# A layer of a hybrid diffusion step on one core: the order in which expert weights are loaded, and four smaller reorderings

## The chip, the cores and the metric

The kernel runs on one NeuronCore of a Trainium2 chip (trn2). The metric is the device time of one execution in microseconds (us). All arithmetic is in 32-bit floats.

## The reference

One layer is computed for 128 context tokens and 512 latent tokens, each of 1024 features. It is an attention sublayer and then a mixture of 16 experts, with a modulation (six vectors of 1024 from a conditioning vector and `w_ada`) around both. Cut to what matters here:

```
def expert_choice_moe(h, w_router, w_gate, w_up, w_down):
    cap = CAPACITY_FACTOR * T // N_EXPERTS          # 64 latent, 16 context tokens for each expert
    logits = jnp.einsum('btd,de->bte', h, w_router, preferred_element_type=jnp.float32)
    aff = jax.nn.softmax(logits, axis=-1)
    g, idx = lax.top_k(jnp.swapaxes(aff, 1, 2), cap)
    xg = jax.vmap(lambda hb, ib: hb[ib])(h, idx)
    a = jnp.einsum('becd,edf->becf', xg, w_gate)
    u = jnp.einsum('becd,edf->becf', xg, w_up)
    y = jnp.einsum('becf,efd->becd', jax.nn.silu(a) * u, w_down) * g[..., None].astype(h.dtype)
    return (each token's rows of y, added up)

def ffn_sublayer(...):
    h = modulate(x, g_pre_ffn, shift, scale)
    return x + gate * rms_norm(expert_choice_moe(h, ...), g_post_ffn)
```

The attention has 16 query heads of 64: eight of group A (all keys, normed and rotated queries) and eight of group B (a window of neighbours and a learned sink). Gate, up and down are 1024x1024 for each expert, 4.2 MB each and 201 MB in all.

## The kernel before, in words

The program writes out by hand what each engine does in order; semaphores tie the engines together. PE is TensorE, ACT ScalarE, DVE VectorE, POOL GpSimd and SP the queue that issues most transfers. Tokens are in five tiles of 128: tile 0 is context, 1 to 4 are latent.

*Projection.* Fifteen passes (three windows of `w_in` by five tiles) make keys, values and queries. PE projects (line 655), turns the result in four blocks (`turn_qk`, L673), ACT copies the high part (`high_part`, L1155) and DVE subtracts it for the low part (`low_part`, L1497). Pass 14 is rotated late, by `rotate_last`.

*Attention.* 80 head units, 40 of group A (`u` from 0) and 40 of group B (from `A_UNITS` = 40; tile 0 comes first). A unit is: scores on PE (L704), `maxima` on DVE (L1569, L1576), exponentials on ACT (L1175), the division on DVE (L1675, L1676), `turn_probs` on PE (L738), `copy_pT` on ACT (L1269) and, each two units, `values` on PE (L760). Between the units of group B, PE does the output projection of the tile before (L809), the turning of the new rows (L822) and the router's logits, `route_logits` (L838). The router's weights times the modulation, `wrm`, are made by DVE at unit 2 (L1684).

*Gap.* The rest of the last tile's projection, then the choice of tokens: DVE finds each expert's 64 and 16 best (L1710 to L1713), POOL gathers their rows, PE turns them (`turn_rows_c`, `turn_rows_l`, L933). `keep_busy` is products whose results nobody reads. The context products of expert 0 come first, from weights loaded since attention's end.

*Experts.* Ring slots 0 to 5 hold two halves of 2 MB each of gate, up and down; slots 6 and 7 hold the gate of each second expert, so a gate is double buffered and up and down are not. PE goes up(e), gate(e+1), down(e), and each half is a context product (L966) and a latent product (L954) in four strips of 32 columns. SP refills a slot when PE has used it, in the order of its own program, and blocks at each wait:

```
def refill(e, kind, odd=False):
    used = ((gate_a, gate_b), (up_a, up_b), (down_a, down_b))[kind]
    for half in (0, 1):
        sp.wait_ge(used[half], e - 1 if kind == 0 else e)
        expert_weight(e, kind, half, SLOTS + half if odd else 2 * kind + half)
```

DVE weighs the result, POOL adds it to the sums in memory by an indirect transfer with addition.

*Tail.* SP reads the sums of the first 15 experts, DVE gates them (L1859), ACT squares them (L1354), POOL takes the root (L2032, L1923), DVE adds the tile (`add_x1`, L1864) and SP stores it. The last expert's rows go another way: `add_last` (L1871), `gain_last` (L1876), a product over the parts on PE (L1091), `mean_last` (L1880), a root, `rows_last_c` (L1887) and `rows_last_l` (L1893), and two indirect writes by POOL (L2039, L2043), which end the kernel.

## Time and profile before

| | us |
|---|---|
| three runs | 947.54, 947.57, 952.59 |
| median | 947.57 |
| the profiled execution | 948.19 |
| its span, first to last instruction | 946.2 |

Busy in the span: PE 884.3 us, the weight load beside it 442.2, DVE 365.8, ACT 216.5, POOL 102.6. The granted TensorE clock is 0.986 of full over the span. Busy time of PE is modelled: a product is shown from its start for a fixed time, so small waits hide in it, and the weight load's own waits (PEld) show them better. A slice of the page is 23.65 us.

### The profile page before, as it was taken

To read this page: it belongs to the slowest core of one execution; us is meant where nothing else is said; L and a number is where in the kernel's file an instruction comes from. 1 tells how busy PE (TensorE), PEld (TensorE's weight loads), DVE (VectorE), ACT (ScalarE), POOL (GpSimd) and SP (SyncE) were. 2 spreads that over 40 slices of the span, in tenths; PEclk is the share of its full clock that TensorE was granted. 3 is DMA by queue.
4 is the path that set the end of the run, shared out by engine and by line. 5 is a ranking of instruction groups with operands and counts; after the bars stand their busy time and mean duration, and the time that the engine had idled before them with its cause. 6 is when DMAs were issued, how large, how long until landed. Compare 5 with 4: busy or idle time off the path is not lost. (4 is left out here: it accounts for less than half of the span.)

```text
span 946.2 us, 19909 instructions
## 1 busy us (share of the span) xinstructions
PE 884.3 (93%) x8641; PEld 442.2 (47%) x8641; DVE 365.8 (39%) x977; ACT 216.5 (23%) x528; POOL 102.6 (11%) x137
## 2 busy tenths in 40 slices
PE   3999998899899999779999999999999999999984
PEld 3544444777656665533444443443444443433431
DVE  4255635888766766811112021121113120210126
ACT  3132223666645653400000000000000000000012
POOL 2021200000000000100110111011101101110225
PEclk9999999999999999899999999999999999999998
DMA  9997532300001116969999999999999999999983
GB/s 337 351 367 279 212 144 96 122 2 1 2 1 46 45 46 239 414 242 405 398 396 411 397 398 403 404 397 397 411 397 397 396 410 398 398 407 391 359 321 151
DMA packets 77717, 269.31 MB, mean 285 GB/s; under 512 B 6208, under 2 KB 9984, under 8 KB 77632
## 3 DMA queue, kind: packets, MB, share of 16 engines
q1 hardware_dynamic: 72384, 251.42, 67.8%
q0 software_dynamic: 4160, 13.90, 5.1%
q10 hardware_dynamic: 1088, 2.74, 0.7%
q8 instruction: 68, 1.11, 0.5%
q14 instruction: 17, 0.14, 0.0%
HBM read 252.06 MB, written 15.99 MB: 283 GB/s over the span
## 5 line engine op out<-in xcount | busy, mean ns | idle before, releaser
L954 PE MATMUL ps<-ring,reg 128*32 128x512 f32 x1792 | 201.6, 592 | 0.0
L1812 DVE TENSOR_SCALAR mod<-ps,kt 64x512 f32<-64x512 f32 x30 | 22.5, 750 | 255.9 <-PE ps L954 255.7
L954 PEld LDWEIGHTS ps<-ring,reg 128*32 128x32 f32 x1792 | 59.1, 110 | 111.8 <-issue 103.3
L966 PE MATMUL ps<-ring,values_in 128*32 128x256 f32 x1536 | 93.6, 386 | 4.0 <-issue 2.9
L1325 ACT ACTIVATE reg<-ps 128x256 f32<-128x256 f32 x16 | 6.1, 384 | 366.6 <-PE ps L1006 354.1
L954 PE MATMUL ps<-ring,kt 128*32 128x512 f32 x768 | 86.8, 592 | 0.0
L809 PE MATMUL ps<-ring,reg 128*128 128x512 f32 x160 | 76.4, 604 | 0.0
L966 PEld LDWEIGHTS ps<-ring,values_in 128*32 128x32 f32 x1536 | 50.0, 112 | 54.1 <-issue 24.8
L655 PE MATMUL ps<-ring,reg_qt 128*128 128x512 f32 x160 | 70.6, 594 | 0.0
L966 PE MATMUL ps<-ring,reg 128*32 128x256 f32 x1024 | 60.9, 379 | 2.5 <-DMA ring<-in_w_down 1.9
L1269 ACT ACTIVATE ring<-ps 128x640 f32<-128x640 f32 (+3 forms) x80 | 44.4, 555 | 72.5 <-PE ps L738 69.9
L738 PE MATMUL ps<-ident,ring 128*128 128x128 f32 x288 | 47.7, 285 | 14.0 <-DVE ring L1676 7.7
L1971 POOL TENSOR_TENSOR small<-mhalf 128x1 f32<-128x1 f32 x31 | 9.5, 306 | 460.1 <-DVE kt L1815 426.7
L1175 ACT ACTIVATE ring<-ps,small 128x640 f32<-128x640 f32 (+3 forms) x80 | 51.0, 638 | 7.9 <-DVE small L1576 7.9
L738 PEld LDWEIGHTS ps<-ident,ring 128*128 128x128 f32 x288 | 33.8, 144 | 37.2 <-issue 19.0
L966 PEld LDWEIGHTS ps<-ring,reg 128*32 128x32 f32 x1024 | 33.0, 110 | 36.8 <-issue 12.9
L954 PEld LDWEIGHTS ps<-ring,kt 128*32 128x32 f32 x768 | 25.4, 110 | 46.8 <-issue 42.8
L655 PEld LDWEIGHTS ps<-ring,reg_qt 128*128 128x128 f32 x160 | 29.6, 190 | 34.7 <-issue 34.7
L760 PE MATMUL ps<-ring,values_in 128*64 128x128 f32 x576 | 40.3, 280 | 0.6 <-ACT ring L1269 0.6
L809 PEld LDWEIGHTS ps<-ring,reg 128*128 128x128 f32 x160 | 28.5, 189 | 24.7 <-issue 24.0
L1676 DVE TENSOR_SCALAR ring<-ring,small 128x640 f32<-128x640 f32 (+3 forms) x80 | 36.8, 460 | 2.8
L631 PE MATMUL ps<-ring,reg_qt 128*128 128x512 f32 x80 | 35.9, 596 | 1.3 <-ACT reg_qt L1122 1.3
(235 smaller groups left out, 1000.7 us busy)
## 6 DMA issues: line engine op xcount, KB each, us to landing
ring<-in_w_up SPq DMA_DIRECT2D x32, 2048.0 KB, 22.7
ring<-in_w_down SPq DMA_DIRECT2D x32, 2048.0 KB, 22.8
ring<-in_w_gate SPq DMA_DIRECT2D x16, 2048.0 KB, 21.6
reg_qt<-in_w_gate SPq DMA_DIRECT2D x16, 2048.0 KB, 22.9
ring<-in_w_ada SPq DMA_DIRECT2D x12, 2048.0 KB, 12.2
reg<-in_x_sample SPq DMA_DIRECT2D x8, 512.0 KB, 6.5
ring<-in_w_in SPq DMA_DIRECT2D x2, 2048.0 KB, 14.1
ring<-in_w_out SPq DMA_DIRECT2D x2, 2048.0 KB, 10.0
```

The source lines that it names most:

```text
L631: last = pe.matmul(projected(t), hT[:, c, t * P:(t + 1) * P], w[:, c, :], start=(c == 0), stop=(c == KC - 1))
L655: last = pe.matmul(projected(i), hT[:, c, t * P:(t + 1) * P], w[:, c, :], start=(c == 0), stop=(c == KC - 1))
L738: last = pe.transpose(two[2][:, b * P:(b + 1) * P], probs[:, u % 3, b * P:(b + 1) * P], ident[:, :])
L760: last = pe.matmul(ps[64 * hh:64 * hh + 64, bank, 0:P], v, pT[:, k % 2, hh, n * P:(n + 1) * P], start=(n == 0), stop=(n == len(blocks) - 1))
L809: last = pe.matmul(out_at(o)[:, n, :], attnT[:, c, t * P:(t + 1) * P], unit_at(wout_units[c // 4], 4)[:, c % 4, n * 512:(n + 1) * 512], st ...
L954: last = pe.matmul(o[64 * n + r:64 * n + r + 32, :], x(4 * hf + j, r), w[:, j, n * HALF:(n + 1) * HALF], start=(hf == 0 and j == 0), stop= ...
L966: last = pe.matmul(o[32 * q:32 * q + 32, :], x(c), w[:, j, q * QUART:(q + 1) * QUART], start=(c == 0), stop=(c == KC - 1))
L1175: act.activation(dst, scores_of(u), ACT.Exp, bias=negm[:, b:b + 1], scale=DH ** -0.5, accum_out=den[:, b:b + 1]).then_inc(exp_done, 1)
L1269: act.activation(pT[:, k % 2, u % 2, 0:n], two[2][:, 0:n], ACT.Copy).then_inc(pT_ready, 1)
L1676: dve.tensor_scalar(probs[:, u % 3, 0:n], probs[:, u % 3, 0:n], rden[:, b:b + 1], None, ALU.mult)\
L1812: dve.tensor_scalar(put_l[:, n * HALF:(n + 1) * HALF], ps[rows, 3, :], g_l[rows, e:e + 1], None, ALU.mult)
L1971: pool.tensor_tensor(held, mhalf[:, 0:1], mhalf[:, 1:2], ALU.add).then_inc(held_ops, 1)
```

## The change

- SP's order: up(e), down(e), gate(e+2) in place of up(e), gate(e+2), down(e).
- Router: the logits are made in four partial sums, with the router's weights (padded to 32 columns) stationary and the tokens moving, each sum in its own strip of 32 columns; ACT copies the parts (`copy_parts`) and one product with a folded identity adds and turns them (`route_merge`). The tables for it are made by DVE at unit 44 and not at unit 2; two products of gains go from unit 4 to unit 14.
- First unit: the maxima, exponentials and division of unit 0 go into projection pass 13, its turning ahead of the last `turn_qk`; the low part and rotation of the last pass go one unit later.
- Gap: more `keep_busy`, the affinities of the last tile turned before the context rows, `turn_rows_l(0)` between the two down products of context.
- Tail: POOL takes roots of three and of two tiles at once; DVE's order changes.

```
@@ SP @@
                     refill(pair * 2 + odd + 1, 1)
+                    refill(pair * 2 + odd + 1, 2)
                     refill(pair * 2 + odd + 3, 0, odd=not odd)
-                    refill(pair * 2 + odd + 1, 2)
             for e in range(E - 3, E):
                 refill(e, 1)
+                refill(e, 2)
                 if e + 2 < E:
                     refill(e + 2, 0, odd=True)
-                refill(e, 2)
@@ PE, projection and first units @@
                 if i == 3 * TILES - 2:
                     scores(0)
+                    turn_qk(3 * TILES - 2)
+            turn_probs(0)
+            scores(1)
             turn_qk(3 * TILES - 1)
             spread_shift()
-            scores(1)
@@ PE, router @@
-                    last = pe.matmul(dst, h2T[:, c, t * P:(t + 1) * P],
-                                     wrm[:, (KC * cond + c) * E:(KC * cond + c + 1) * E], start=(c == 0),
-                                     stop=(c == KC - 1))
-                last.then_inc(router_done, 1)
+                    q = c % 4
+                    last = pe.matmul(bank[32 * q:32 * q + 32, 0:P], wrm_by[:, cond, c, :], h2T[:, c, t * P:(t + 1) * P],
+                                     start=(c < 4), stop=(c >= 4))
+                last.then_inc(parts_done, 1)
+            def route_merge(o):
+                bank = (out_at(o) if o < TILES - 1 else out_at(o - 1))[:, 1, :]
+                pe.wait_ge(parts_copied, o + 1)
+                pe.matmul(bank[:, P:P + E], logit_parts, merge, start=True, stop=True).then_inc(router_done, 1)
@@ PE, gap @@
-            pe.wait_ge(logits_ready, TILES)
+            keep_busy(3, 6)
+            turn_aff(4)
             turn_rows_c(0)
-            turn_aff(4)
+            keep_busy(3, 10)
...
             turn_rows_c(1)
-            keep_busy(3, 4)
-            turn_lists()
             pe.wait_ge(silu_done, 1)
             weight_in(2, 0)
             product_c(2, GC[:, QUART:], context_of(0))
+            keep_busy(3, 4)
+            turn_lists()
...
             product_c(SLOTS, GC[:, 0:QUART], context_of(1)).then_inc(up_c, 1)
-            pe.wait_ge(xc_ready, 2)
-            turn_rows_l(0)
+            keep_busy(3, 3)
...
             product_c(4, YC[:, 0:QUART], acts_c)
+            pe.wait_ge(xc_ready, 2)
+            turn_rows_l(0)
             weight_in(5, 0)
             product_c(5, YC[:, 0:QUART], acts_c)
@@ ACT @@
+            def copy_parts(o):
+                bank = (out_at(o) if o < TILES - 1 else out_at(o - 1))[:, 1, :]
+                act.wait_ge(parts_done, o + 1)
+                if o:
+                    act.wait_ge(router_done, o)
+                act.activation(logit_parts, bank[:, 0:P], ACT.Copy).then_inc(parts_copied, 1)
...
             square_x1_half(1)
+            copy_parts(4)
             normalise_x1(4)
             store_rows(4)
@@ DVE, units @@
+                if i == 3 * TILES - 2:
+                    maxima(0)
                 if i >= 1:
                     low_part(i - 1)
+                if i == 3 * TILES - 2:
+                    low_part(i)
+                    normalise(0)
...
+                if u:
+                    normalise(u)
                 if u == 0:
+                    low_part(3 * TILES - 1)
+                if u == 1:
                     rotate_last()
...
-                if u == 2:
+                if u == A_UNITS + 4:
+                    dve.wait_ge(scores_done, A_UNITS)
+                    link(dve.memset(kt[:, 2048:2048 + 2 * KC * CPAD], 0.0))
+                    fold = lambda q: ident[:, 32 * q:32 * q + E]
+                    link(dve.tensor_tensor(merge, fold(0), fold(1), ALU.add))
+                    link(dve.tensor_tensor(merge, merge, fold(2), ALU.add))
+                    dve.tensor_tensor(merge, merge, fold(3), ALU.add).then_inc(router_set, 1)
...
-                if u == 4:
+                if u == 14:
                     dve.wait_ge(mod_ready, N_MOD + 2)
@@ DVE, tail @@
             for t in range(1, TILES):
                 gate_sum(t)
-                add_x1(t - 1)
+            add_x1(0)
             add_last(1)
-            add_x1(TILES - 1)
             gain_last(1)
+            add_x1(1)
             mean_last(1)
+            add_x1(2)
+            add_x1(3)
             add_last(0)
+            add_x1(4)
             gain_last(0)
-            rows_last_c(0)
             mean_last(0)
-            rows_last_c(1)
-            rows_last_c(2)
             rows_last_l()
-            rows_last_c(3)
+            for q in range(4):
+                rows_last_c(q)
@@ POOL @@
-            for t in range(TILES):
-                pool.wait_ge(f_squared, t + 1)
-                pool.tensor_scalar(msf[:, t:t + 1], ssf[:, t:t + 1], EPS, None, ALU.add).then_inc(f_mean, 1)
-                root(rsf[:, t:t + 1], msf[:, t:t + 1], 1, f_mean, f_rstd, t + 1)
+            for k, (a, b) in enumerate(((0, 3), (3, TILES))):
+                pool.wait_ge(f_squared, b)
+                pool.tensor_scalar(msf[:, a:b], ssf[:, a:b], EPS, None, ALU.add).then_inc(f_mean, 1)
+                root(rsf[:, a:b], msf[:, a:b], b - a, f_mean, f_rstd, k + 1)
```

## Rows read from the trace of the kernel before

**Rows 1.** The page: busy us by engine; DMA's busy tenths and GB/s in 40 slices.

```profile
PE 884.3 (93%) x8641; PEld 442.2 (47%) x8641; DVE 365.8 (39%) x977; ACT 216.5 (23%) x528; POOL 102.6 (11%) x137
...
DMA  9997532300001116969999999999999999999983
GB/s 337 351 367 279 212 144 96 122 2 1 2 1 46 45 46 239 414 242 405 398 396 411 397 398 403 404 397 397 411 397 397 396 410 398 398 407 391 359 321 151
```

**Rows 2.** Waits of the weight load, 770 to 890 us: total us, times, longest.

```profile
PEld ps L966 <- DMA ring<-in_w_down: 6.9, 7, 1.7
PEld ps L966 <- DMA ring<-in_w_up: 5.2, 8, 0.9
```

**Rows 3.** The same view, 430 to 770 us.

```profile
PEld ps L966 <- DMA ring<-in_w_down: 0.3, 1, 0.3
```

**Rows 4.** SP's issues in order of time, 434 to 448 us: start us, us.

```profile
434.40 0.38 SPq L476 DMA_DIRECT2D ring<-in_w_up  x1
...
447.88 0.37 SPq L476 DMA_DIRECT2D ring<-in_w_down  x1
```

**Rows 5.** DMA issues from 423 to 424 us: count, KB, us to landing.

```profile
ring<-in_w_gate SPq DMA_DIRECT2D x1, 2048.0 KB, 7.7
```

**Rows 6.** DMA issues from 434 to 435 us.

```profile
ring<-in_w_up SPq DMA_DIRECT2D x1, 2048.0 KB, 13.9
```

**Rows 7.** DMA issues from 753 to 754 us.

```profile
ring<-in_w_up SPq DMA_DIRECT2D x1, 2048.0 KB, 27.1
```

**Rows 8.** Weight loads in order of time around the first route.

```profile
303.75 0.19 PEld L838 LDWEIGHTS ps<-wrm,reg 128*128 128x128 f32 x1 [0.24 <-issue]
...
305.77 0.51 PEld L738 LDWEIGHTS ps<-ident,ring 128*128 128x128 f32 x4
```

**Rows 9.** Weight loads in order of time, 18 to 21.5 us (modulation).

```profile
18.27 1.86 PEld L560 LDWEIGHTS ps<-ring,reg 128*32 128x32 f32 x64 [0.33 <-issue]
20.33 0.53 PEld L604 LDWEIGHTS ps<-ident,reg 128*128 128x128 f32 x5 [0.20 <-issue]
```

**Rows 10.** The same view in an expert, 596 to 599 us.

```profile
596.56 0.20 PEld L1006 LDWEIGHTS ps<-ident,reg 128*128 128x128 f32 x2 [0.84 <-issue]
```

**Rows 11.** DVE in order of time, 149 to 170 us.

```profile
159.63 1.39 DVE L1497 TENSOR_TENSOR q_b<-ps,q_b 64x512 fp32r<-64x512 f32 x2 [3.32 <-ACT q_b L1155]
...
163.90 0.55 DVE L1676 TENSOR_SCALAR ring<-ring,small 128x640 f32<-128x640 f32 x1
...
169.53 0.48 DVE L1684 SCALAR_TENSOR_TENSOR wrm<-wr,colmod 128x128 f32<-128x128 f32 x2
```

**Rows 12.** DVE's groups by line, 0 to 20 us: busy us, mean ns, idle before.

```profile
L1381 DVE MEMSET mod<- 128x1536 f32 x1 | 1.3, 1338 | 1.1 <-PEq L2087 1.1
```

**Rows 13.** Busy time by stretch: PE, PEld, DVE, ACT, POOL, clock, DMA share, GB/s.

```profile
252.00:257.00 5.00, 4.03 (x19) 2.26 (x18) 4.62 (x18) 2.80 (x12) 0.00 (x0) 1.00 0.00 0
```

**Rows 14.** PE in order of time, 149 to 170 us.

```profile
164.51 1.33 PE L738 MATMUL ps<-ident,ring 128*128 128x128 f32 x5 [3.84 <-DVE ring L1676]
...
168.09 1.12 PE L738 MATMUL ps<-ident,ring 128*128 128x128 f32 x5 [0.33 <-DVE ring L1676]
```

**Rows 15.** PE in order of time, 402 to 421 us.

```profile
411.58 3.41 PE L966 MATMUL ps<-reg_qt,values_in 128*32 128x256 f32 x32 [4.36 <-DMA reg_qt<-in_w_gate]
...
416.80 3.66 PE L966 MATMUL ps<-ring,reg 128*32 128x256 f32 x64 [0.56 <-ACT reg L1325]
```

**Rows 16.** POOL in order of time, 918 to 944 us.

```profile
929.67 1.40 POOL L1923 TENSOR_TENSOR small<-small,mhalf 128x1 f32<-128x1 f32 x1
...
936.97 0.55 POOL L1923 TENSOR_TENSOR small<-small,mhalf 128x1 f32<-128x1 f32 x1 [1.50 <-DVE small L1880]
...
938.85 0.44 POOL L1971 TENSOR_TENSOR small<-mhalf 128x1 f32<-128x1 f32 x1 [1.33 <-issue]
```

**Rows 17.** PE in order of time, 924 to 938 us.

```profile
925.23 7.05 PE L954 MATMUL ps<-ring,reg 128*32 128x512 f32 x64
```

**Rows 18.** DVE in order of time, 918 to 944 us.

```profile
937.96 0.75 DVE L1893 SCALAR_TENSOR_TENSOR reg_qt<-reg_qt,small,reg 128x512 f32<-128x512 f32 x1
```

More of the change, by code:

```diff
@@ L706, in scores, with turn_probs @@
                 last.then_inc(scores_done, 1)
+            def turn_probs(u):
+                g, h, t = HEAD_UNITS[u]
+                pe.wait_ge(probs_ready, u + 1)
+                if u == 0:
+                    pe.wait_ge(mod_ready, N_MOD + 2)
+                    pe.wait_ge(qkT_ready, 3 * TILES - 1)
+                    pe.wait_ge(qkT_act, 3 * TILES - 1)
+                if u:
+                    pe.wait_ge(pT_ready, u)
+                for b in range(key_count(g, t) // P):
+                    last = pe.transpose(two[2][:, b * P:(b + 1) * P], probs[:, u % 3, b * P:(b + 1) * P], ident[:, :])
+                last.then_inc(probs_turned, 1)
             for i in range(3 * TILES):
@@ L875, in _ @@
                 if o >= 2 and j == 7:
-                    route_logits(o - 2)
+                    route_parts(o - 2)
+                if o >= 3 and j == 1:
+                    route_merge(o - 3)
             turn_probs(n_units - 1)
             values(n_units // 2 - 1)
-            project_out(4, 0, 6)
+            project_out(4, 0, 2)
+            route_merge(2)
+            project_out(4, 2, 6)
             for o in range(3):
@@ L1282, in _ @@
                     copy_x1(o - 2, j - 5)
-                if o >= 3 and j == 1:
+                if o >= 3 and j == 0:
+                    copy_parts(o - 3)
+                if o >= 3 and j == 2:
                     exp_logits(o - 3)
@@ L1295, in _ @@
             square_half(0)
+            copy_parts(3)
             exp_logits(3)
```

140 lines of the change are left out of this document (68 added, 72 removed).

## The prediction

> **What bounds the kernel now.** I read the page first. TensorE (PE) is busy 93% of the span and the DMA slices stand at 9 from slice 19 on, so from about 425 us to 890 us two resources look full at once [rows 1]. The reader has to find out which one waits for the other. The waits of the weight load say it: from 770 to 890 us it stood 6.9 us for down matrices and 5.2 us for up matrices, 12.1 us in 15 waits [rows 2]. Before 770 us the same view shows 0.3 us for down and nothing for up [rows 3]. So transfers fall behind slowly, and late in the loop they are what PE waits for.
>
> The queue's own issues and their times to landing show how. The load issued at 423 to 424 us into an empty queue took 7.7 us; the second half of the first up matrix, issued at 434.4 us, took 13.9 us; one issued at 753 to 754 us took 27.1 us, and it lands at the first of the long waits [rows 4 to 7]. A slot is therefore needed again about 27 us after it was freed, and the backlog grows into that. A half matrix is 2.1 MB; at the 405 GB/s of the slices it takes 5.2 us. The expert loop is thus a chain of transfers that never pauses from 426 us on, and its end is its start plus bytes over rate. This decides what every other part of the change is worth: work saved ahead of the loop moves its start and counts in full; the order inside it counts only where it makes the chain pause, or where it lets PE finish later than its last transfer.
>
> **The change part by part.** My sum is against the profiled execution, 948.19 us (span 946.2 us and 2.0 us around it); it stands 0.6 us above the median of 947.57 us.
>
> *Weight order.* Before: up(e), gate(e+2), down(e). After: up(e), down(e), gate(e+2). SP waits for the slot of down(e), freed one PE step later than that of the gate; now both halves of the gate wait behind it on SP, and the next up behind them. A gate matrix has two experts' time in hand, so its delay by about 16 us costs PE nothing. The next up has the same transfers ahead of it in both orders, and so lands at the same time if the queue never runs dry. The waits for down go, but PE then comes to the next up earlier and waits there longer for the same landing: the 6.9 us are not won, they change their name. The queue can run dry once. The second half of up(1) lands at 434.4 + 13.9 = 448.3 us; the first down is issued at 447.88 us, when its slot comes free [rows 4, 6]. Now the gate's two halves cover the stretch behind it; after the change nothing does. A load into an empty queue needed 7.7 us where 5.2 us are transfer, so 2.5 us pass before data flow at its full rate: 447.88 + 7.7 = 455.6 us, against the 448.3 + 5.2 = 453.5 us at which the next transfer ends now. That is 2.1 us of pause, or 1.6 us if part of the 2.5 us is the telling of the landing, which I take. Ends: 0 and 2.6. It can't repeat: a pause puts the queue behind PE, and the next down is issued with that much more in front of it.
>
> *Router.* A route is now eight products with 128x128 weights and 16 columns, and takes PE from 303.75 to 305.77 us, 2.02 us [rows 8]. It becomes eight products with 128x32 weights in four column strips and 128 columns, a copy of the parts on ScalarE, and one merging product. The same form stands in the modulation part: 64 weight loads from 18.27 us to the next group at 20.33 us, 2.06 us, of which 0.31 us is the change of shape [rows 9]; 16 of them take 0.44 us, with the change 0.75 us. The merge is one eighth of the old route, 0.25 us. Each route saves 1.27 us and gives 0.25 us back. Three routes and two merges stand inside attention, where PE is the bound from 257 us on: -3.8 + 0.5 = -3.3 us. The last two lie behind attention, where transfers already run (below), and count nothing. The copy is 0.3 us of ScalarE beside PE work; the merge is placed two head units later. If each change of shape costs the 0.84 us that the weight load stood idle behind a strip product in the loop instead of 0.31 us [rows 10], the part gives -1.7 us. The Trainium skill's page "TensorEngine Tiling (Array Packing)", section "Key Properties", says that changing the tiling mode drains TensorE, which speaks against small packed products; it gives no time, and both rows show such a drain, so the sum lies between the two.
>
> *Building the router's weights.* VectorE (DVE) did it at the third unit of group A (0.48 us [rows 11]) and now does it at the fifth unit of group B, with a clearing of 128x512 in front and three linked additions. The memset of 1536 columns took 1.3 us [rows 12], so 0.45 us here; each small linked addition is near 0.2 us; together 0.45 + 0.6 + 0.6 = 1.65 us. That place is the context tile, with short units: PE is busy only 4.03 of 5 us there, and DVE 4.62 [rows 13]. About 0.6 us of it finds idle DVE time, +1.0 us stays. Ends 0 and 1.65.
>
> *First unit.* Now PE stands 3.84 us before it turns the first probabilities at 164.51 us, because DVE does both low parts (from 159.63 us, 1.39 us each, when ScalarE's high part is ready) before it normalises at 163.90 us [rows 11, 14]. The change normalises unit 0 in the projection's last pass, so the turn moves to about 158 us. But unit 1 then needs: spread shift on PE (after the last q turn, about 160.9 us), the copy of the bias, the maxima 0.82, exponentials 0.9, high part 1.2, low part 1.39, maxima 0.82, normalise 0.7 and the last rotation 2.05 us, in one line over two engines: 169 us, where PE turns the last q and then the probabilities of unit 1, which stood at 168.09 us [rows 14]. The wait is moved behind unit 0 and not removed. DVE loses 0.48 us at unit 2 [rows 11] and two gain products (an estimate from it: 0.8 us) at unit 4, which come back at unit 14, where it has little slack. I take +1.2 us, ends -1 and +2.5.
>
> Attention thus ends 1.1 us earlier: 1.2 + 1.0 - 3.3.
>
> *Gap.* The loads of expert 0 and of the second gate run without a pause from the end of attention; their landing at 411.58 us ends PE's wait of 4.36 us [rows 15]. It moves with attention's end alone. Warming products before it, the earlier product and the later store of the last rows (ScalarE now copies router parts in front, some 1.5 us) all lie under it. Behind it the turn of the latent rows now stands between the two context products, which start at 416.80 us [rows 15]: those start 0.3 us earlier, and 0.95 us of turning stands on PE before the first latent product. +0.7 us, ends -0.5 and +1.3. The loop's transfers start 0.4 us earlier.
>
> *Tail.* The root of each tile is two GpSimd (POOL) operations; the power is 1.40 us long beside DVE's work and 0.55 us when DVE is idle [rows 16]. Ten become four. Of the skill, "GPSIMD Engine Reference", section "Specifications", says that GpSimd shares its SBUF interfaces with VectorE and contends with two-input instructions: the trace agrees, with 1.40 against 0.55 us [rows 16]. The roots are ready by 929 us instead of 933. But DVE's order now puts the mean of the last context rows, which needs a PE product behind all down products (their last group starts at 925.23 us, lasts 7.05 us and so ends at 932.3 us [rows 17]), before three of the five additions of 1.28 us. From 932.8 us: 2 x 1.28 + 0.75 (last sum) + 1.28 + 0.69 + 0.2 + root 0.6 + 0.75 = 939.7 us, against 938.7 us now (937.96 + 0.75 [rows 18]). The fifth tile's store starts at 937.5 and takes 2.7 us, so POOL's last writes start at 940.2 instead of 938.85 us [rows 16]. +1.4 us, ends -1 and +2.
>
> Sum: -1.1 + 0.7 + 1.6 + 1.4 = +2.6 us, or 950 us beside the median.
>
> **The rivals.** *The early parts gain and nothing is lost:* no pause, first unit at 0, gap and tail at 0: -3.3 + 1.0 and 1 us for the first unit: 944.5 us. For it: each of my losses is a chain of estimates. *The order itself is worth something:* if the waits came from the order and not from bytes over rate, the 6.9 us for down vanish: 950 - 7 = 943 us, and with those for up 938 us. Against it: the backlog's steady growth. *Slower, the queue runs dry at each expert:* if down's slot always comes free after the last up has landed, 14 pauses of 1.6 us give 22 us, half of them 961 us. It decides from the moment at which down's issue comes later than the landing of the up before it; they are 0.4 us apart at the first expert [rows 4, 6], and by the growing times to landing the distance grows. *The changed order does nothing*, each load being hidden as before: 948.5 us.
>
> **How the numbers follow.** Forecast (947.5 to 953 us) 0.5; order does nothing 0.13; early gains 0.17; order worth something 0.12; slower 0.08. The range of 944 to 955 us leaves out the slow case, most of the order's worth and the far ends of two parts. What a measurement here can tell from no change is 1%, 9.5 us: below 938 us 0.05, above 957 us 0.07, between 0.88.
>
> **What would show it.** Right: waits for down near zero and more for up in the same stretch; a short dip in GB/s near 449 us; a route under 0.8 us; attention's end about 1 us earlier; POOL's last writes later. Wrong: PE without waits for weights, dips at every expert, or a first unit of group A with no new wait at unit 1. I would be wrong most if the transfer rate depended on how many loads stand in the queue, which no row here can show.

## The result, and the profile after

The changed kernel takes 957.28 us (median of 4 runs, 956.37 to 958.10) beside 948.84 us for the kernel before: ratio 1.0075, 95% interval 1.0047 to 1.0104, so 4.5 to 9.9 us slower. The forecast was 950.0 us, 944 to 955 us. The profiled execution of the changed kernel took 956.66 us (span 954.5 us), 8.3 us of span more than before. One run of an experiment below (before, new tail) took 2364.01 us and is left out of its median.

The page's rows on PE, PEld, DVE and POOL busy time and on DMA, as in [rows 1]:

```profile
PE 886.7 (93%) x8689; PEld 439.8 (46%) x8689; DVE 366.9 (38%) x981; ACT 217.0 (23%) x533; POOL 98.3 (10%) x131
...
DMA  9997532300001116968999999999999999999984
GB/s 338 340 347 296 216 137 99 117 2 1 2 0 46 45 45 245 415 225 353 387 396 410 398 398 399 409 398 398 405 401 399 397 410 398 398 403 402 352 305 157
```

PE is busy 2.4 us longer; the rest of the 8.3 us is waiting. Slice 18, counted from 0, shows it: 353 GB/s where before had 405. The waits of the weight load, first from 430 to 770 us, then from 770 to 900 us (total us, times, longest; the lines on DMA):

```profile
PEld ps L984 <- DMA ring<-in_w_up: 7.9, 8, 2.0
...
PEld ps L984 <- DMA ring<-in_w_up: 9.2, 8, 2.1
```

No wait for a down matrix is left, and those for up are 17.1 us, against 12.4 us for up and down together [rows 2, 3]. They changed their name, and grew.

The span is best cut at events that both kernels have. A turn is the start of its weight load (the rows of the products begin 0 to 0.4 us later), and a landing is the issue plus its time to landing:

| stage, us | before | after | difference |
|---|---|---|---|
| start to the turn of unit 2's probabilities | 170.07 | 172.90 | +2.8 |
| to unit 44's | 80.08 | 80.06 | 0 |
| to unit 48's | 6.10 | 8.42 | +2.3 |
| to the first gate matrix's issue | 106.23 | 103.88 | -2.3 |
| to gate(2)'s issue | 61.46 | 62.72 | +1.3 |
| to the landing of up(2), first half | 51.48 | 54.89 | +3.4 |
| to the landing of the last up | 427.88 | 427.86 | 0 |
| to the end | 42.90 | 43.80 | +0.9 |

The two zeros say as much as the rest: nothing lost is made good, and the expert loop, once past its start, runs at the same pace in both orders.

**The pause.** SP's issues in order of time (start us, us from first to last):

```profile
435.40 3.41 SPq L478 DMA_DIRECT2D ring<-in_w_up  x2
451.90 3.81 SPq L478 DMA_DIRECT2D ring<-in_w_down  x2
455.99 0.93 SPq L478 DMA_DIRECT2D reg_qt<-in_w_gate  x2
```

The busy time by stretch of 1 us (its last two columns are DMA share and GB/s):

```profile
449.00:450.00 1.00, 1.00 (x16) 0.32 (x12) 0.00 (x0) 0.34 (x1) 0.00 (x0) 1.00 0.94 377
450.00:451.00 1.00, 1.00 (x16) 0.33 (x12) 0.00 (x0) 0.00 (x0) 0.00 (x0) 1.00 0.18 70
451.00:452.00 1.00, 1.00 (x12) 0.26 (x8) 0.00 (x0) 0.00 (x0) 0.00 (x0) 1.00 0.07 29
452.00:453.00 1.00, 1.00 (x16) 0.32 (x12) 0.00 (x0) 0.00 (x0) 0.00 (x0) 1.00 0.20 20
453.00:454.00 1.00, 1.00 (x16) 0.34 (x12) 0.00 (x0) 0.00 (x0) 0.00 (x0) 1.00 0.74 193
454.00:455.00 1.00, 1.00 (x12) 0.26 (x8) 0.00 (x0) 0.00 (x0) 0.00 (x0) 1.00 1.02 389
```

What is missing from 410 GB/s in the five stretches from 450 us on is 340 + 381 + 390 + 217 + 21 = 1349 KB, or 3.3 us of transfer. The second half of up(1), issued at 438.43 us, lands after 13.6 us, at 452.0 us. Finer stretches show what the queue does before and behind that:

```profile
450.10:450.60 0.50, 0.50 (x12) 0.13 (x4) 0.00 (x0) 0.00 (x0) 0.00 (x0) 1.00 0.18 74
450.60:451.60 1.00, 1.00 (x12) 0.26 (x8) 0.00 (x0) 0.00 (x0) 0.00 (x0) 1.00 0.12 49
451.70:452.90 1.20, 1.20 (x16) 0.35 (x12) 0.00 (x0) 0.00 (x0) 0.00 (x0) 1.00 0.00 0
452.90:453.40 0.50, 0.50 (x12) 0.16 (x8) 0.00 (x0) 0.00 (x0) 0.00 (x0) 1.00 1.03 106
```

From 450.1 us on only three of the 16 DMA engines still move bytes (a share of 0.18), then two (0.12), until 451.6 us; the others have finished their part of the load. The landing is told 0.4 us behind the last packet of the slowest engine, and so 1.9 us after most of the queue has run dry. The down matrix, issued at 451.90 us, when its slot comes free, starts its first packets 1.05 us later, and they take 0.6 to 0.7 us each where 0.16 us is usual (a full share at 106 GB/s in the last row). Counted in bytes the chain stood from about 450.1 to 453.4 us, and not from one landing to the next issue. In the kernel before, the same load had ended on 13 engines at 446.4 us and landed at 448.33 us, but there the gate's halves were already queued behind it.

The Trainium skill, "DMA: Bandwidth & Descriptors", the table "Where the ~2 µs actually goes", in a section on transfers that GpSimd issues, says that most of a transfer's fixed cost comes after its last byte, until the target has confirmed it. The traces of these loads, which SP issues, do not agree: 0.4 us lie behind the last packet and 1.05 us ahead of the first.

**The first unit.** DVE in order of time, lines left out between:

```profile
161.57 0.19 DVE L1710 COPY rbias<-ps 128x32 f32<-128x32 f32 x1 [2.84 <-PE ps L691]
...
164.72 1.39 DVE L1532 TENSOR_TENSOR q_b<-ps,q_b 64x512 fp32r<-64x512 f32 x2 [2.03 <-ACT q_b L1175]
...
167.72 0.68 DVE L1519 TENSOR_TENSOR reg<-reg 128x512 f32<-128x512 f32 x1
```

PE in the same stretch:

```profile
158.78 0.71 PE L720 MATMUL ps<-ident,ring 128*128 128x128 f32 x5
...
160.85 0.61 PE L691 MATMUL ps<-ident,small 16*128 16x16 f32 x4
...
169.86 1.12 PE L675 MATMUL ps<-ident,reg 128*128 128x128 f32 x4 [5.35 <-DVE reg L1526]
170.77 1.27 PE L720 MATMUL ps<-ident,ring 128*128 128x128 f32 x5
```

Unit 0's probabilities are turned at 158.78 us in place of 164.51 us [rows 14]. Then DVE waits 2.84 us for the spread shift (PE L691), 2.03 us for ScalarE's high part, and rotates last; PE stands 5.35 us until it may turn the last q. Unit 1 comes behind that turn, at 170.77 us, against 168.09 us [rows 14]: the wait has moved behind unit 0 and grown.

**Unit 44 and what follows.** DVE builds the tables from 252.09 us to 253.52 us (1.43 us), and units 45 to 47 are 0.7 us later. Then this (PEclk is the third column from the right):

```profile
256.00:258.00 2.00, 1.35 (x8) 0.70 (x8) 1.83 (x9) 1.19 (x5) 0.00 (x0) 0.98 0.00 0
258.00:260.00 2.00, 2.00 (x5) 1.43 (x5) 1.86 (x8) 1.14 (x5) 0.00 (x0) 0.50 0.00 0
260.00:262.00 2.00, 2.00 (x5) 0.72 (x5) 1.33 (x5) 0.00 (x0) 0.00 (x0) 0.67 0.03 8
```

PE's clock falls to 1.2 GHz (half) just as the 512-column products begin, after a stretch in which PE was busy 1.1 to 1.35 of every 2 us; that is the other 1.6 us. Before had the full clock there, 1.00 in each stretch of 2 us from 244 to 262 us.

**A route** in the weight load's order of time:

```profile
308.46 0.19 PEld L814 LDWEIGHTS ps<-ring,reg 128*128 128x128 f32 x1 [0.24 <-issue]
309.41 0.38 PEld L844 LDWEIGHTS ps<-reg,kt 128*32 128x32 f32 x16 [0.76 <-issue]
309.99 0.42 PEld L720 LDWEIGHTS ps<-ident,ring 128*128 128x128 f32 x4 [0.20 <-issue]
```

The sixteen loads take 0.38 us, but 0.76 us of idle stands ahead of them, at the change into the strip shape, where other loads have 0.24. From the last 512-column load to the next unit's loads it is 1.53 us (308.46 to 309.99), against 2.45 us before (303.32 to 305.77): a route saves 0.92 us.

**The tail.** PE, then DVE, in order of time:

```profile
932.76 7.05 PE L972 MATMUL ps<-ring,reg 128*32 128x512 f32 x64
939.74 0.38 PE L1111 MATMUL ps<-small,gqk 128*128 128x1 f32 x2
944.19 0.59 PE L1111 MATMUL ps<-small,wr 128*128 128x1 f32 x2 [4.07 <-ACT reg_qt L1394]
```

```profile
940.16 0.16 DVE L1928 TENSOR_SCALAR small<-ps 128x1 f32<-128x1 f32 x1 [1.13 <-PE ps L1111]
940.24 2.48 DVE L1912 SCALAR_TENSOR_TENSOR ring<-ring,small,reg 128x1024 f32<-128x1024 f32 x2
942.64 0.74 DVE L1919 SCALAR_TENSOR_TENSOR reg_qt<-ps,kt,reg 128x512 f32<-128x512 f32 x1
```

The mean of the context rows at 940.16 us waits for PE, and two additions of 1.24 us stand between it and the latent sum. From the start of the last down group to the end it is 21.8 us, against 21.0 before.

### The profile page after: what moved, and what is told of

It reads as the page before. It is cut to its first block and busy times, and to the rows that moved or that the text cites. A ratio compares the mean times of both kernels' runs of the same rounds, so it can differ in the third digit from the quotient of the medians.

```text
span 954.5 us, 20012 instructions
## 1 busy us (share of the span) xinstructions
PE 886.7 (93%) x8689; PEld 439.8 (46%) x8689; DVE 366.9 (38%) x981; ACT 217.0 (23%) x533; POOL 98.3 (10%) x131
## 5 line engine op out<-in xcount | busy, mean ns | idle before, releaser
L972 PE MATMUL ps<-ring,reg 128*32 128x512 f32 x1792 | 201.6, 592 | 0.0
L972 PEld LDWEIGHTS ps<-ring,reg 128*32 128x32 f32 x1792 | 58.5, 110 | 112.5 <-issue 103.9
L972 PE MATMUL ps<-ring,kt 128*32 128x512 f32 x768 | 86.9, 592 | 0.0
L984 PEld LDWEIGHTS ps<-ring,values_in 128*32 128x32 f32 x1536 | 48.4, 110 | 57.4 <-DMA ring<-in_w_up 17.1
L657 PE MATMUL ps<-ring,reg_qt 128*128 128x512 f32 x160 | 70.6, 595 | 0.0
L720 PE MATMUL ps<-ident,ring 128*128 128x128 f32 x288 | 47.4, 283 | 10.3 <-ACT ring L1296 6.0
L972 PEld LDWEIGHTS ps<-ring,kt 128*32 128x32 f32 x768 | 25.5, 110 | 46.6 <-issue 42.7
L984 PE MATMUL ps<-reg_qt,values_in 128*32 128x256 f32 x512 | 32.5, 397 | 6.0 <-DMA reg_qt<-in_w_gate 6.0
```

What stands on the lines that cost most here:

```text
L657: last = pe.matmul(projected(i), hT[:, c, t * P:(t + 1) * P], w[:, c, :], start=(c == 0), stop=(c == KC - 1))
L720: last = pe.transpose(two[2][:, b * P:(b + 1) * P], probs[:, u % 3, b * P:(b + 1) * P], ident[:, :])
L972: last = pe.matmul(o[64 * n + r:64 * n + r + 32, :], x(4 * hf + j, r), w[:, j, n * HALF:(n + 1) * HALF], start=(hf == 0 and j == 0), stop= ...
L984: last = pe.matmul(o[32 * q:32 * q + 32, :], x(c), w[:, j, q * QUART:(q + 1) * QUART], start=(c == 0), stop=(c == KC - 1))
```

## The experiments

Times are medians; each set of experiments had its own runs of the kernel before beside it (medians 949.2 to 949.8 us). "Ratio" is to these, with its 95% interval.

| kernel | us | ratio |
|---|---|---|
| changed, old weight order | 956.2 | 1.0063 (1.0039 to 1.0088) |
| before, new weight order | 953.2 | 1.0035 (1.0018 to 1.0052) |
| changed, first cycle in old order | 958.7 | 1.0098 (1.0069 to 1.0126) |
| changed, tables early | 958.7 | 1.0096 (1.0066 to 1.0127) |
| changed, old first unit | 955.2 | 1.0054 (1.0032 to 1.0075) |
| changed, old gap | 954.5 | 1.0053 (1.0032 to 1.0074) |
| changed, old tail | 958.8 | 1.0104 (1.0081 to 1.0126) |
| before, router alone | 947.6 | 0.9980 (0.9967 to 0.9993) |
| the same, once more | 946.5 | 0.9969 (0.9957 to 0.9981) |
| router and new first unit | 948.8 | 0.9994 (0.9982 to 1.0006) |
| before, new tail | 950.5 | 1.0010 (0.9996 to 1.0024) |
| before, new gap | 950.4 | 1.0012 (0.9997 to 1.0027) |
| before, idle products | 951.7 | 1.0031 (1.0018 to 1.0044) |
| router and idle products | 949.2 | 0.9998 (0.9984 to 1.0012) |

**The weight order put back, and put in alone.**

```diff
                     refill(pair * 2 + odd + 1, 1)
-                    refill(pair * 2 + odd + 1, 2)
                     refill(pair * 2 + odd + 3, 0, odd=not odd)
+                    refill(pair * 2 + odd + 1, 2)
```

> The changed kernel, with the weight order put back (gate matrix of two experts on ahead of the down matrix); router, first unit, gap and tail stay changed. Theory 1 (one pause): in the changed kernel the DMA queue stood once, at the first down matrix of the loop; from the second expert on both orders move bytes at one rate. So the stretch from the issue of gate(2) to the landing of the second half of the last up matrix goes from 459.3 us back to about 456.2, 3.1 less, all of it before expert 2, and the time is about 954.2. The waits for the down matrices come back and those for up go. Rival A (the order acts in every expert): the transfers of each expert get faster or slower, and the difference of the two kernels' landings grows or shrinks from expert to expert; the stretch changes by 5 us or more, in steps. Rival B (the loop's start costs nothing of its own, its end is only carried late by what came before): the stretch stays at 459 and the time at 957.

> The kernel before, with the weight order alone changed. Theory 1 (one pause): gate(2)'s issue stays at 424 us, the first down matrix stops the queue once, and the last up matrix lands some 3.1 us later than before's 880.1; time about 951.9 (before 948.8). Rival A (the order acts in every expert): 5 us or more, growing expert by expert. Rival C (it is the late start of the loop in the changed kernel, and not the order, that opened the pause): with the gap's work as before, the step from up(1) to down(1) stays near 5 us, and the time is 949.

From gate(2)'s issue to the landing of the last up matrix the changed kernel with the old order took 479.7 us, before with the new order 482.9 us. (The expectation gives 456 and 459 for this stretch: the same difference of 3.1 to 3.3 us, counted to an earlier matrix.) Over all profiled executions: 479.1 to 479.7 us in the old order (ten), 482.5 to 483.1 us in the new (seven). Nothing else in this case repeats so closely. The time of the new order alone agrees, 1.0035, or 3.3 us (1.7 to 4.9). All of it is lost before up(2): the step from up(2) to the last up is 428.3 us in the one and 428.0 us in the other. That supports the single pause, and speaks against a cost at each expert (rival A) and against the late start as its cause (rival C). With the old order put back the median fell by only 1 us, less than the 3.1 expected. The ratios to before, 1.0063 and 1.0075, have intervals of 3.7 to 8.4 and 4.5 to 9.9 us, so a gain of 3.3 us is neither shown nor excluded by these times. What its one profile adds stands under the tail.

**Only the first cycle in the old order.**

```diff
             refill(2, 0)
-            with sp.Fori(0, E // 2 - 2) as pair:
+            refill(1, 1)
+            refill(3, 0, odd=True)
+            refill(1, 2)
+            refill(2, 1)
+            refill(2, 2)
+            refill(4, 0)
+            with sp.Fori(1, E // 2 - 2) as pair:
```

> The changed kernel with the first cycle alone in the old order (up 1, gate 3, down 1), the second and all later ones in the new (up, down, gate). Theory 1: the pause stood at the first down matrix alone, since its buffer comes free only when the product of expert 0 with it is done; a gate matrix moved ahead of it fills the time, and as later the queue is behind the buffers, no pause comes in its place: stretch from gate(2)'s issue to the last up matrix about 456.3, time about 954.2. Rival D (the pause only moves to the next cycle): down(2) stands as long as down(1) did, the stretch stays at 459 and the time at 957.

Theory 1 and rival D are each half right. The stretches of this kernel:

```profile
447.00:450.00 3.00, 3.00 (x33) 0.91 (x29) 0.00 (x0) 0.61 (x2) 0.00 (x0) 1.00 1.03 410
450.00:453.00 3.00, 3.00 (x33) 0.91 (x29) 0.00 (x0) 0.26 (x1) 0.00 (x0) 1.00 1.02 407
...
483.00:486.00 3.00, 3.00 (x48) 1.39 (x44) 0.00 (x0) 0.00 (x0) 0.00 (x0) 1.00 0.78 257
```

The hole at 450 us is closed, and one opens at 483 us, where down(2) is issued (482.99 us). It is smaller: the whole stretch is 481.1 us, so half of the 3.3 us is won. The pause comes at the first place where a down matrix has no gate in front of it; how long it is depends on how far the queue is behind by then. The time, 958.7 us, did not fall to the 954.2 us expected. In the profiled execution the tail, with half clock just ahead of its last group, took 47.1 us from the landing of the last up matrix, against 43.8 us.

**The tables of the router made early.**

```diff
-                if u == A_UNITS + 4:
-                    dve.wait_ge(scores_done, A_UNITS)
-                    link(dve.memset(kt[:, 2048:2048 + 2 * KC * CPAD], 0.0))
+                if u == 2:
...
-                    last = pe.matmul(bank[32 * q:32 * q + 32, 0:P], wrm_by[:, cond, c, :], h2T[:, c, t * P:(t + 1) * P],
+                    last = pe.matmul(bank[32 * q:32 * q + E, 0:P], wrm_by[:, cond, c, :], h2T[:, c, t * P:(t + 1) * P],
```

> The changed kernel with the router's tables made at unit 2 in a buffer of their own, with strips of 16 columns and no zeroed padding, so no memset, no sums and no scaling at unit 44. Theory 2 (tables and the clock): units 45 to 47 were 0.7 us late by those 1.43 us of VectorE, and the longer idle of TensorE there brought its clock down to half at 257.9 to 261.3 us, which cost 1.6 us more; both go, so that unit 48's turn comes 2.3 us earlier against that of unit 44, and the time is about 955.0. Rival E (the clock falls anyway, the context tile leaves TensorE idle in both kernels): 0.7 us back, time 956.6. Rival F (off the path): nothing back, 957.

Units 44 to 48 took 6.09 us, as before's 6.10, so the 0.7 us and the 1.6 us were both gone. But the kernel was not faster: 958.7 us, where 955.0 was expected. Its profiled execution had half clock at 23 to 27 us and again ahead of the tail, was 1.5 us later at unit 2, 1.5 us longer in the gap and 2.7 us longer in the tail. And the kernel with the old weight order put back, which has the tables where the changed kernel has them, took 6.86 us over the same units: 0.76 us for the tables and no half clock. So the tables cost 0.76 us, and the clock need not fall with them.

**Both kernels again, unchanged.**

> The kernel before, not changed at all, profiled once more. Theory 7 (a part of what one execution shows is the luck of where TensorE's clock falls): the spells of half clock lie elsewhere than in the first profile (which had none between 240 and 265 us and only 3.4 us in the gap), and the stages in which they lie are longer by 1.5 to 3 us: turn of unit 48 near 258.5 in place of 256.25, or gate(2)'s issue near 425.5 in place of 423.9. Rival K (order of instructions fixes the clock): the spells within 0.5 us of the first profile's.

> The changed kernel, not changed at all, profiled once more. Theory 7: the spell at 257.9 to 261.3 may be absent, and one may come at 927 to 935 in the tail, after which the span from the last up matrix's landing to the end is 46 to 47 us in place of 43.8; the pause at the first down matrix (gate(2)'s issue to the landing of the first half of up(2) 54.9 us, 51.5 before) is there again. Rival K: everything within 0.5 us of the first profile.

Each is a single execution. The kernel before took 953.15 us (span 951.1 us), 4.95 us more than in its first profile and within the 945.7 to 953.7 us of its other runs. Its stretches:

```profile
252.00:258.00 6.00, 5.34 (x15) 2.73 (x14) 5.54 (x22) 2.98 (x12) 0.00 (x0) 0.60 0.01 3
...
411.00:418.00 7.00, 3.30 (x32) 1.38 (x32) 0.00 (x0) 0.00 (x0) 0.00 (x0) 0.69 0.90 363
...
922.00:929.00 7.00, 4.62 (x38) 2.03 (x34) 5.18 (x6) 3.27 (x7) 1.85 (x5) 0.76 1.01 380
```

Here the half clock falls on units 46 to 49, where it fell on nothing before, and costs 2.6 us by unit 56; it stays longer in the gap, which takes 63.1 us and not 61.5. The changed kernel took 960.74 us, above its four timed runs (956.37 to 958.10), with such a spell at 931 to 935 us that its first profile did not have; the pause was there again (55.1 us from gate(2)'s issue to the first half of up(2)). The order of instructions is the same and the spells are not: rival K falls. Of the sixteen profiles without idle products ten have one on units 46 to 49: six of the seven with the tables at unit 44, and four of the nine with them elsewhere. These few don't settle whether the changed kernel draws it more often. The Trainium skill, "TensorE: Matmul & The Clock Gate", says in its Part 1 that the gate's watch runs free and does not begin with the kernel. The two profiles of one kernel agree with that: the spells lie elsewhere, and 4.95 us are between the spans.

For the comparison this means that a stage's difference between two single profiles is a cost only where it repeats.

**The first unit.**

```diff
-                    turn_qk(3 * TILES - 2)
-            turn_probs(0)
-            scores(1)
             turn_qk(3 * TILES - 1)
             spread_shift()
+            scores(1)
```

(and the high and low parts, maxima, copy and normalisation on ScalarE and DVE moved back to match)

> The changed kernel with the first unit's order put back (unit 0's scores behind the last rotations, unit 0's probabilities not brought forward). Theory 3: the turn of unit 2's probabilities came 2.8 us late in the changed kernel (3.0 and 4.0 to 4.3 in three variants of it), although unit 0's came 6 early, since the work brought forward stands ahead of the rotations and low parts that unit 1 waits for, and TensorE's half clock falls on it; both go with the old order: unit 2's turn within 0.4 of before's 170.07, time about 954.8. Rival G (the start of the profiled run is late by itself, in a landing of the first weights): unit 2 stays 2 to 3 us late, 957.

> The kernel before with the router (tables made early) and the first unit's new order; weight order, gap and tail old. Theory 3: unit 2's turn at 172.7 to 174.4 in place of 170.0 to 170.7, nothing of it made good later: median 3 above that of the router alone, some 950.6. Rival P (the loss is made good before the weights' first issue, since attention has idle time): median of the router alone, 947.6.

Unit 2 was turned at 170.00 us with the old order, as theory 3 says. Over the profiled executions it comes at 170.0 to 170.7 us with the old order and at 172.7 to 172.9 us with the new. Four more had a spell of half clock at 23 to 28 us and so started 1.1 to 1.7 us late (171.8 us twice with the old order, 174.0 and 174.4 with the new). The router with the new first unit came at 171.8 us, but its unit 0 was 1.1 us early too; from unit 0 to unit 2 it took the same 14.5 us as the changed kernel. The times: 955.2 us without the new first unit, and in one set of runs 948.8 us with it against 946.5 us for the router alone, 2.3 us, where theory 3 had 3. Rival P falls.

**The gap.**

```diff
-            keep_busy(3, 6)
+            pe.wait_ge(logits_ready, TILES)
+            turn_rows_c(0)
             turn_aff(4)
-            turn_rows_c(0)
-            keep_busy(3, 10)
```

(and the turn of the latent rows and of the lists back to their places)

> The changed kernel with the old order of TensorE's work between attention and experts. From the issue of the first gate matrix to that of gate(2) before took 61.5 us, the changed kernel 62.7, its variants 63.4 and 64.2, but before with the new weight order alone 63.0 as well, its half clock there 6.9 us long as in all of these, where before had 3.4 us of it. Theory 4 (the 1.3 us are the clock's, not the order's): about 63.0 with a half clock of 6.9 us, time 957, as the changed kernel. Rival H (the order costs them): 61.5, time 956.0.

> The kernel before with TensorE's order between attention and experts alone changed. Theory 9 (the new order costs 2.0: issue of the first gate matrix to that of gate(2) 63.3 on the mean of seven executions against 61.3 of seven with the old): 62.7 to 64.2 in the profile, median some 951.2. Rival O (only the clock's spells set it): 61.5 or 63 and the median of before, 949.2.

From the first gate matrix's issue to that of gate(2): the old order 59.4 to 63.1 us in ten executions (mean 61.5), the new 62.0 to 64.2 us in eight (mean 63.2). Put back in the changed kernel it gave 60.7 us and a time of 954.5 us, below both expectations, the largest gain of the parts put back; alone on the kernel before it cost 1.1 us, with an interval from -0.3 to 2.6. So the new order costs something, by the stages some 1.1 to 1.6 us and not the 2.0 of theory 9, though the times alone don't separate it from nothing. The two kernels' half clock differs here each time. The kernel before, then before with the new gap alone (PEclk is the third column from the right):

```profile
390.00:397.00 7.00, 4.07 (x41) 2.24 (x43) 6.11 (x24) 4.19 (x9) 1.29 (x2) 0.55 1.03 416
411.00:418.00 7.00, 5.85 (x66) 3.39 (x70) 2.74 (x5) 0.38 (x1) 1.03 (x2) 0.76 0.51 204
...
390.00:397.00 7.00, 5.59 (x55) 4.93 (x57) 5.75 (x24) 4.06 (x12) 1.29 (x2) 1.00 1.02 411
411.00:418.00 7.00, 4.58 (x40) 2.30 (x40) 0.42 (x1) 0.00 (x0) 0.00 (x0) 0.59 0.89 359
```

With the old order all ten executions had a spell between 388 and 400 us, and eight of them 3.4 to 3.5 us of half clock at a time behind 404 us. With the new order, which has more idle products, none of the eight had the first spell, and all had one of 6.8 to 6.9 us between 410 and 420 us, over the end of the wait for the gate and the first products behind it. The two old-order executions that also had so long a spell there took 63.0 and 63.1 us, as long as the new order's mean. So most of what the order costs seems to come by way of the clock, though two executions are few: theory 4 is right that the 1.3 us are the clock's, and wrong that the order has no part in them. PE behind the last landing in the changed kernel:

```profile
414.04 3.64 PE L984 MATMUL ps<-reg_qt,values_in 128*32 128x256 f32 x32 [5.99 <-DMA reg_qt<-in_w_gate]
...
421.52 1.09 PE L951 MATMUL ps<-ident,reg 128*128 128x128 f32 x8
```

The 1.09 us of turning the latent rows now stand between the two context products; before, they stood ahead of the context products' release. At equal half clock the first latent product starts 9.8 to 10.3 us behind the landing with the new order (three executions) and 9.7 and 9.9 us with the old (two).

**The tail.**

```diff
-                dve.wait_ge(f_rstd, 1 if t < 3 else 2)
+                dve.wait_ge(f_rstd, t + 1)
...
-            add_x1(0)
...
+                add_x1(t - 1)
```

(with the roots one tile at a time again)

> The changed kernel with the old tail. From the landing of the last up matrix to the end before took 42.9 us, before with the new weight order 43.3, though that had TensorE at half clock at 926 to 930; the changed kernel took 43.8 and, with such a half clock, 46.4 to 47.1 in three variants. Theory 5 (the new tail leaves the half clock on its path and the old one does not, and costs 0.9 without it and 3.2 to 3.8 with it): 43.0 to 43.3 whatever the clock does, time 954.5 to 956. Rival I (the 46 to 47 are late transfers of the last down matrix): 46 again in some runs, time 957.

> The kernel before with the tail's order alone changed. Theory 8 (the new tail costs 0.6 without a spell of half clock at 922 to 935 and 3.3 with one, which came in some half of the executions): median 1 to 3 us above before's 949.2, and in the profile the span from the last up matrix's landing to the end 43.8, or 46 and more if the spell is there. Rival N (the 46 to 47 belong to how late the changed kernel reaches the tail): 43.0 to 43.5 and the median of before.

The old tail in the changed kernel did not make it faster (958.8 us, four runs from 956.4 to 960.5); alone on before the new tail cost 1.0 us, with an interval from -0.4 to 2.3. The profiles are clearer if the tail is counted from the start of the last down group (PE L972 above). With the new order it takes 21.8 to 22.1 us in all eight executions, however late that group starts and with or without half clock ahead of it. With the old order it takes 19.1 to 19.7 us in the four executions where the group before it ran at half clock; where it ran at full clock, 21.0 to 21.2 us in four and 19.6 and 22.1 us in two. Both expectations had the wrong measure: it is not that the new tail lets the spell on its path. The old one is paced by DVE's additions, with slack for a late PE, and takes back up to 1.9 us; the new one hangs on PE's last product and takes back nothing. In the second profile of the kernel before:

```profile
931.54 7.04 PE L954 MATMUL ps<-ring,reg 128*32 128x512 f32 x64
938.51 0.38 PE L1091 MATMUL ps<-small,gqk 128*128 128x1 f32 x2
941.26 0.38 PE L1091 MATMUL ps<-small,wr 128*128 128x1 f32 x2 [2.37 <-ACT reg_qt L1359]
```

Between the two small products are 2.75 us here, and 4.45 us in the new tail. It bears on the weight order too, which put back gave 1 us in the time and not 3: the one profile of that kernel drew half clock at 23 to 27 and at 928 to 931 us, and was 1.1 us later than the changed kernel's first at unit 2 and 2.7 us longer in the tail. Whether its other six runs did the same is not shown.

**The router alone.**

> The kernel before with the router alone changed: strips of 16 columns, tables made at unit 2 in a buffer of their own, the copy and the merge as in the changed kernel; all else old. Theory 6: each route saves 0.93 us and each merge gives 0.25 back, 3 routes and 2 merges lie inside attention: its end, and with it everything behind, comes 2.3 us earlier; routes 4 and 5 lie in the gap, where they hide or save up to 0.7 each; time 946.2 to 946.9 where before has 949.2. Rival J (what is won in attention is lost in the gap, where the merge waits for the copy of the parts on the path to the lists): 949.

> The router alone on the kernel before, as in the run of that name: 2.3 us less than before without a difference in the clock's spells, 947 to 948, ratio 0.998.

947.6 and 946.5 us: 1.9 and 2.9 us less than before, both intervals below 1, the first 0.7 us above what was expected and the second 0.5 us below. It is the fastest version here and beats both kernels. From unit 48 to the first gate's issue it takes 103.8 us in its second profile, against 106.23. Rival J falls.

**Idle products against the half clock.**

```diff
+                if A_UNITS + 2 <= u < A_UNITS + 8:
+                    keep_busy(6, 4)
```

> The kernel before with four idle 128-column products added in each of units 42 to 47, at the end of TensorE's work for the unit, where it waits for the probabilities. Theory 7: they keep TensorE from the half clock that some executions showed at 254 to 261 us (2.3 to 3.2 us lost by it), so that the turn of unit 48 lies at 256.3 to 256.8 in each; the profile shows no half clock between 245 and 265, and the median falls by up to 1, as not all executions had the spell. Rival L (the products stand in the way of the units' own work): 6 units by up to 0.25 us, 1.5 us slower, 950.7. Rival M (they are too few): the spell is there.

> The kernel before with the router alone changed (tables made early) and the same idle products in units 42 to 47. Theories 6 and 7: unit 48's turn at 256.3 to 256.8, first gate matrix issued 2.3 us ahead of before's 362.5, at 360.2 to 360.7; time 946 to 947, the fastest of all here. Rival L: 949. Rival M: the router alone again, 947.6.

No profile with them shows half clock at 245 to 265 us, and both were slower than without: 951.7 and 949.2 us. PE's stretches in the first:

```profile
252.00:256.00 4.00, 4.00 (x36) 3.34 (x33) 3.21 (x16) 2.26 (x11) 0.00 (x0) 1.00 0.00 0
```

They keep the clock and cost 2.5 us (unit 48's turn at 258.7 us, against 256.25), as much as a spell costs when it comes. Theory 7 is right on the clock and wrong on the time; rival L, with 1.5 us forecast, is nearer.

## Why the prediction was wrong, by its steps

- *What bounds the kernel*: right. The loop is a chain of transfers, its end is its start plus its bytes; from up(2) to the last up the two kernels are equal to 0.1 us, and all profiles but that of the first cycle lie within 427.5 to 428.4 us. The waits changed their name.
- *Weight order, +1.6 us (0 to 2.6)*: mechanism and place right, one pause at the first down matrix; 3.3 us measured. The step that failed is "the second half of up(1) lands at 448.3 us; the first down is issued at 447.88": I took the landing as the moment at which the queue runs dry. In the changed kernel 13 of the 16 DMA engines were dry at 450.1 us, 1.9 us before the landing, because two of them ended 1.5 us after the others and the landing is told 0.4 us behind the last. From 450.1 us to the issue are 1.8 us, from there to the first packets 1.05 us, and these are 0.5 us slower than usual: 3.3 us. The 0.5 us that I took for the telling of the landing is 0.4 us, and the 2.0 us that I left ahead of full rate are 1.5 us. What was missing is the 1.9 us between the end of most engines, 446.4 us in the kernel before, and the landing at 448.3 us: read so, its rows would have given 447.88 + 1.5 - 446.4 = 3.0 us.
- *Router, -3.3 us*: -2.3 in the stages, -1.9 and -2.9 in the times of the router alone. The saving per route is 0.92 us and not 1.27 (three routes and two merges give -2.3); the step that failed is the 0.31 us for the change of shape, read where 32-column strips give way to another small group. Behind a 512-column product the gap is 0.95 us from load to load where 0.43 is usual. The end of the range (-1.7) held it. The Trainium skill, "TensorEngine Tiling (Array Packing)", "Key Properties", says that a change of mode drains the engine; the trace agrees, with 0.76 us of standing.
- *Tables, +1.0 us*: 0.76.
- *First unit, +1.2 us (to 2.5)*: 2.3 to 2.7. The line over the engines was right, and DVE's waits for the spread shift and the high part are in it: it gave 169 us for the turn of the last q, which came at 169.86. The step that failed is setting these 169 us against the 168.09 us of unit 1's turn: unit 1 stands behind the last q, whose turn takes another 0.9 us, so it came at 170.77. Late by 0.9 as forecast, 0.9 for the line and 0.9 for the turn make the 2.7.
- *Gap, +0.7 us (to 1.3)*: 1.1 alone. The turn between the context products was priced; the longer half clock behind the landing, which came with the new order in all eight executions, was in no term.
- *Tail, +1.4 us (to 2)*: 0.8 on the profile, 1.0 in the time alone; the queue behind the context rows' mean was as forecast. Not foreseen: the old tail took back up to 1.9 us of a late PE.
- *Sum*: +2.6 forecast; the parts as measured alone give 3.3 - 2.4 + 0.8 + 2.3 + 1.1 + 1.0 = +6.1 us, within the 4.5 to 9.9 of the whole. What is left to its middle (7.1 us) may be the tail's lost slack; the runs don't settle it. Every term but the tables and the tail was off to the slow side, and three of them near or over the end of their own range.
- *The rivals*: "dry at each expert" did not happen. The case that came, all parts a little worse, had no place of its own, and the range of 955 us was made as if the terms' errors would cancel. The clock's spells, 5 us between two executions of one kernel, were in no term. The 3.5 us between the forecast sum and the measured one are several steps: the pause 1.7, the first unit 1.1, the router 0.9 and the gap 0.4, less 0.2 for the tables and 0.4 for the tail.

Open: whether the changed attention draws the half clock at units 46 to 49 more often, why two DMA engines end a load later than the others, and why the old tail did not help the changed kernel in its times.

## What to carry to other kernels

When a chain of transfers may pause, look at the rate and the share of busy DMA engines, and count from where they fall to where the next load has them full again, not from landing to issue: a landing is told by the slowest engine, when most of the queue may already be dry. A buffer that is needed late is worth loading early where it fills the time until an earlier one comes free, and an order that looks idle is often the slack that takes up a late engine. Before pricing a stage from one profile, profile the same kernel twice: what does not repeat is not a cost of the order. And test parts alone: the one good part here was hidden under five poor ones.

## What the runs showed of the hardware

- The granted clock of TensorE fell to half (1.2 GHz) at other places in two executions of one program, and the spans differ by 4.95 us; a spell on units 46 to 49 cost 0.8 to 2.6 us, by its length and place.
- A 2 MB load into an empty queue starts its first packets 1.03 to 1.06 us after its issue, in every profile here.
- The 16 DMA engines do not end a queued load together: in the changed kernel 13 had finished up(1) 1.9 us before its landing was told and the last two 0.4 us before it.
- With the new order of the gap, which has more idle products, the half clock at 388 to 400 us was gone in all eight executions (it was there in all ten with the old order), and a spell of 6.8 to 6.9 us stood at 410 to 420 us. Which of the moved and added products does it was not tested.
- A change from 512-column products to 32-column strips takes 0.95 us from load to load, where 0.43 us is usual.
